# Per-token L2 norms in a delta rule's tables, and a value projection made feature-major

## The reference, cut to what matters

```
q = l2_norm(silu(conv(z_q))) * 128 ** -0.5      # x * rsqrt(sum(x * x) + 1e-6)
k = l2_norm(silu(conv(z_k)))
kk = k @ k.T ;  a_mat = tril(beta * kk * decay, -1) + I
u, w = solve(a_mat, [v * beta, k * beta * exp(gc)])
o = (q * exp(gc)) @ s + (q @ k.T * decay) @ (u - w @ s)
s = s * a_last + (k * exp(gc_last - gc)).T @ (u - w @ s)
y = rms_norm(o_forward + o_backward, g) * silu(gate) @ w_out
```

## Time and profile before

| | us |
|---|---|
| three runs | 3838.85, 3844.15 (median), 3849.88 |
| profiled execution | 3842.82 |
| its span | 3841.0 |

### The profile page before, as it was taken

The page is one execution under the profiler, slowest core; times in us unless marked ns, Lnnn a source line. Parts: engine busy times, 40 slices in busy tenths (PEclk is TensorE's granted clock), DMA queues, the critical chain, the costliest instruction groups (busy, mean ns, idle before and its releaser), DMA issues.

```text
span 3841.0 us, 60563 instructions
## 1 busy us (share of the span) xinstructions
PE 3669.0 (96%) x25450; PEld 2964.8 (77%) x25450; DVE 1940.4 (51%) x3011; ACT 1525.8 (40%) x2592; POOL 841.5 (22%) x829
## 2 busy tenths in 40 slices
PE   7999899999999999999999999999999899999999
PEld 4678787887887667777888788875778688878887
DVE  5656655655444656743344543447565523354343
ACT  5543333433233457634234322235664523343222
POOL 1121232112121225432101121113253211002020
PEclk7999999999999999999999999999999999999999
DMA  6310030032222111111233222220211122322222
GB/s 233 126 51 3 22 69 3 3 121 87 95 99 88 66 39 61 67 45 69 96 108 106 77 99 94 99 72 33 72 61 64 37 99 94 111 87 93 99 99 89
DMA packets 81975, 300.87 MB, mean 78 GB/s; under 512 B 8872, under 2 KB 10024, under 8 KB 81064
## 3 DMA queue, kind: packets, MB, share of 16 engines
q1 hardware_dynamic: 80672, 294.90, 21.8%
q10 hardware_dynamic: 1032, 2.10, 0.5%
HBM read 292.76 MB, written 4.19 MB: 77 GB/s over the span
## 4 chain that ended last, share of the span: by engine, by line
PE 73%; DVE 11%; ACT 6%; issue 5%; POOL 4%; DMA 1%; SPq 0%; DVEq 0%; POOLq 0%; ACTq 0%
PE ps L208 72%; DVE wlo L239 1%; DVE he L247 1%; ACT whi L227 1%; PE ps L213 1%; DVE ac L247 1%; DVE hc L2504 1%; ACT ha L227 1%; POOL p L243 1%; DVE ss L247 1%; ACT wp L228 1%; DVE ha L239 1%; ACT L227 1%; DVE ws L247 1%; DVE sml L1972 1%
## 5 line engine op out<-in xcount | busy, mean ns | idle before, releaser
L239 DVE TENSOR_TENSOR wlo<-wraw,whi 128x1024 fp32r<-128x1024 f32 x537 | 690.5, 1290 | 767.5 <-ACT whi L227 766.9
L208 PE MATMUL ps<-hh,whi 128*128 128x512 f32 x1840 | 729.3, 396 | 7.2 <-ACT hh L227 2.2
L208 PE MATMUL ps<-hh,wlo 128*128 128x512 f32 x1840 | 720.3, 391 | 0.0
L208 PE MATMUL ps<-hl,whi 128*128 128x512 f32 x1840 | 720.3, 391 | 0.0
L227 ACT ACTIVATE whi<-wraw 128x1024 fp32r<-128x1024 f32 x537 | 559.7, 1049 | 214.0 <-PE ps L208 176.9
L208 PEld LDWEIGHTS ps<-hh,whi 128*128 128x128 f32 x1840 | 348.2, 189 | 91.7 <-ACT hh L227 8.7
L208 PEld LDWEIGHTS ps<-hh,wlo 128*128 128x128 f32 x1840 | 347.7, 189 | 73.7
L208 PEld LDWEIGHTS ps<-hl,whi 128*128 128x128 f32 x1840 | 347.9, 189 | 69.8
L208 PE MATMUL ps<-u,u 64*64 64x64 f32 (+1 forms) x6016 | 222.4, 226 | 22.7 <-DVE u L239 16.0
L208 PEld LDWEIGHTS ps<-u,u 64*64 64x64 f32 x6016 | 202.7, 135 | 41.8 <-DVE u L239 18.9
L208 PE MATMUL ps<-gh,wlo 128*128 128x512 f32 x528 | 205.4, 389 | 0.0
(11 more groups left out here) (406 smaller groups left out, 7006.4 us busy)
## 6 DMA issues: line engine op xcount, KB each, us to landing
wraw<-weights SPq DMA_DIRECT2D x537, 512.0 KB, 3.2
x<-xT SPq DMA_DIRECT2D x1, 2048.0 KB, 12.1
bias_lines<-ln ACTq DMA_DIRECT2D x1, 2048.0 KB
x<-xT SPq DMA_DIRECT2D x4, 512.0 KB, 5.3
xmf<-memT SPq DMA_DIRECT2D x2, 1024.0 KB, 4.9
out<-x SPq DMA_DIRECT2D x4, 512.0 KB, 2.6
bias<-bias_lines SPq DMA_DIRECT2D x1, 1536.0 KB, 8.2
con<-consts SPq DMA_DIRECT2D x1, 1379.0 KB, 16.5
```

The costliest lines, as they stand in the source:

```text
L208: self.last, self.open = self.e.matmul(out, lhsT, rhs, start=start, stop=stop, skip_group_check=skip), True
L239: return self.e.tensor_tensor(out, a, b, op)
```

## The change

The norms are no longer applied to queries and keys. `QT`, `KT` and `KM` hold the raw values, and the per-token factors go into tables. With r the reciprocal norm of a key, `beta` (for the values) becomes beta r, `betak` (for the matrix) beta r r, and `nbe` is multiplied by r r. A query's norm is a common factor of its whole output row, and the output is normalized again, so it drops out except beside the epsilon: the sum of squares plus 1e-6, times 128e-6, takes the epsilon's place (`qe`). The sums of the keys' squares are now taken token-major: ScalarE squares the transposed keys out of PSUM, right after it copies them to `KM`, and VectorE reduces them. The powers of a head group's keys are taken together, for 24 columns. The keys' transposes move from step 3 to step 1.

In the window stage the values are projected feature-major, like the keys, copied to `wVT`, and turned by four transposes behind the first scores.

```diff
-    steps = {"q": 3, "k": 4, "v": 2}
+    steps = {"q": 2, "k": 2, "v": 2}
...
@@ pe_chunks
-            elif kind == "v" or step == 3:
+            elif kind != "q":
                 ...
                 K.pe_turn6(z)
-            elif step == 1:
+            else:
                 ... (sums of squares, as before)
-            else:
-                sm = K.sml[("c", *z)]
-                pe.wait_ge(K.pool.at("croot", *z))
-                for m0 in range(0, nt, 4):
-                    b = K.ps.take(pe, "cb", *z, m0)
-                    for m in range(min(4, nt - m0)):
-                        pe.mm(b[:, m * 128:m * 128 + 128], sm[:, m0 + m:m0 + m + 1].broadcast_to([128, 128]), K.con("id"))
-                    pe.mark("cb", *z, m0)
-                pe.also("sml", "c", *z)
@@ pe_turn6
-            pe.wait_ge(K.dve.at("cn", *z, 0), K.dve.at("cn", *z, 4))
+            pe.wait_ge(K.pool.at("cm", *z))
@@ act_chunks
-                if kind != "v":
-                    dst = K.QT[:, i, :] if kind == "q" else K.KT[:, i, :]
+                if kind == "q":
                     act.wait_ge(K.pool.at("cm", *z))
-                    act.a(s[:, 0:nt * 128], dst, ACT.Square).then_inc(act("csq", *z), 1)
+                    act.a(s[:, 0:512], K.QT[:, i, :], ACT.Square).then_inc(act("csq", *z), 1)
...
                     act.cp(dst[:, m0:m0 + mn, i * 128:i * 128 + 128], v).then_inc(act("ct", *z, m0), 1)
+                    if kind == "k":
+                        sq = K.sg[hg][z][:, m0 * 128:(m0 + mn) * 128]
+                        act.a(sq, K.ps[("ct", *z, m0)][:, 0:mn * 128], ACT.Square).then_inc(act("ksq", *z, m0), 1)
@@ dve_chunks (the sums with epsilon and the products "cn" go)
+            elif kind == "q":
+                dve.wait_ge(pe.at("cs", *z), dve.at("qe", 0) if hg else None)
+                dve.ts(K.qsum[:, :, i], K.ps[("cs", *z)][:, 0:4], EPS, ALU.add, 128 * EPS, ALU.mult).then_inc(dve("qsum", hg, i), 1)
+                dve.also("ps", "cs", *z)
+                if i == 3:
+                    K.dve_query_norms(hg)
+            elif kind == "k":
+                dve.wait_ge(K.act.at("ksq", *z, 0), K.act.at("ksq", *z, 4), dve.at("gg"), dve.at("kroot", 0) if hg else None)
+                sq = K.sg[hg][z][:, 0:768].rearrange("p (a b) -> p a b", b=128)
+                dve.e.reduce_sum(K.ksum[:, :, i], sq, AXX).then_inc(dve("ksum", hg, i), 1)
+                dve.also(f"sg{hg}", *z)
+                if i == 3:
+                    dve.wait_ge([dve.at("ksum", hg, j) for j in range(4)])
+                    dve.ts(K.ksum, K.ksum, 1.0, ALU.mult, EPS, ALU.add).then_inc(dve("keps", hg), 1)
+            if (kind, i, step) == ("v", 2, 0):
+                K.dve_key_norms(hg)
@@ pool_chunks (the power and the scaling per item go)
+            elif (kind, i) == ("k", 3):
+                pool.wait_ge(K.dve.at("keps", hg))
+                pool.tt(K.ksum, K.ksum, K.con("mhalf").unsqueeze(2).broadcast_to([128, 6, 4]), ALU.pow).then_inc(pool("kroot", hg), 1)
+    def dve_query_norms(self, hg):      # 4 copies of 64 partitions x 2 x 4 into qe
...
+    def dve_key_norms(self, hg):        # 8 copies of 64 partitions x 2 or 4 x 4 into kroot, then
+        dve.tt(beta, beta, K.kroot, ALU.mult).then_inc(dve("kbeta", hg), 1)
+        dve.tt(nbe, nbe, K.kroot, ALU.mult).then_inc(dve("knbe0", hg), 1)
+        dve.wait_ge(dve.at("knbe0", hg))
+        dve.tt(betak, beta, K.kroot, ALU.mult).then_inc(dve("kbetak", hg), 1)
+        dve.tt(nbe, nbe, K.kroot, ALU.mult).then_inc(dve("knbe", hg), 1)
@@ pool_scan
-                pool.tt(q4(A), q4(E), bcl(K.cols(K.beta, s, hg), 64), ALU.mult).then_inc(pool("eb", *z), 1)
+                pool.tt(q4(A), q4(E), bcl(K.cols(K.betak, s, hg), 64), ALU.mult).then_inc(pool("eb", *z), 1)
@@ dve_osum
-        dve.ts(o[:, 0, hg, j, :], o[:, 0, hg, j, :], 1.0 / 128, ALU.mult, EPS, ALU.add).then_inc(dve("ort", hg, j), 1)
+        dve.stt(o[:, 0, hg, j, :], o[:, 0, hg, j, :], 1.0 / 128, ALU.mult, K.qe[:, hg, j, :], ALU.add).then_inc(dve("ort", hg, j), 1)
@@ pe_window
-        K.projT(("wv", l), [("w_in_2", l, k * 128, slice(o, o + 128)) for k in ks8], 128,
-                [(b[:, c * 128:c * 128 + 128], c == 0) for c in range(4)], h)
+        K.proj(("wv", l), K.win(l, "v", 0), [(ps.take(pe, "wv", l), h)])
...
+            if c == 0:                  # behind the first eight score products' banks
+                b = ps.take(pe, "wvt", l)
+                pe.wait_ge(act.at("wvT", l))
+                for n in range(4):
+                    pe.tr(b[:, n * 128:n * 128 + 128], L.wVT[:, n * 128:n * 128 + 128], K.con("id"))
+                pe.mark("wvt", l)
@@ act_window
-        act.wait_ge(pe.at("wv", l))
-        act.cp(L.wV.rearrange("p a b -> p (a b)"), ps["wv", l]).then_inc(act("wv", l), 1)
+        act.wait_ge(pe.at("wv", l), K.ended("units", l))
+        act.cp(L.wVT, ps["wv", l]).then_inc(act("wvT", l), 1)
         act.also("ps", "wv", l)
+        act.wait_ge(pe.at("wvt", l))
+        act.cp(L.wV.rearrange("p a b -> p (a b)"), ps["wvt", l]).then_inc(act("wv", l), 1)
+        act.also("ps", "wvt", l)
```

More of the change, by code:

```diff
@@ L492, in layout @@
         self.nbe = self.sb("nbe", G, [128, 2, 6, 8])
+        self.qe = self.sb("qe", G + 160, [128, 2, 4, 4])
+        self.ksum = self.sb("ksum", G + 384, [128, 6, 4])
+        self.kroot = self.sb("kroot", G + 408, [128, 2, 6, 4])
+        self.betak = self.sb("betak", G + 480, [128, 2, 6, 8])
+        self.qsum = self.sb("qsum", G + 976, [128, 4, 4])
         self.ea = self.sb("ea", G + 960, [128, 2, 8])
@@ L600, in layout @@
             L.wV = self.sb("wv", M + 2560, [128, 4, 128])
+            L.wVT = self.sb("wvt", M + 9216, [128, 512])
             L.wS = self.ring(f"ws{l}", [self.sb("ws", M + o, [128, 4, 384]) for o in (3072, 4608, 12288)], after_b)
@@ L1264, in dve_chunks @@
                     K.dve_osum(0, i, K.OT[:, i, 1, :])
[L1265 to L1270, removed]
-                dve.also("ps", "cs", *z)
[L1272 to L1279, removed]
+            elif kind == "q":
+                dve.wait_ge(pe.at("cs", *z), dve.at("qe", 0) if hg else None)
+                dve.ts(K.qsum[:, :, i], K.ps[("cs", *z)][:, 0:4], EPS, ALU.add, 128 * EPS, ALU.mult).then_inc(dve("qsum", hg, i), 1)
+                dve.also("ps", "cs", *z)
+                if i == 3:
[10 more added lines that the diff above has]
+                K.dve_key_norms(hg)
             if (hg, kind, i, step) == (0, "q", 2, 1):
@@ L1317, in pool_chunks @@
                     pool.also(f"ac{hg}", *z)
[L1318 to L1325, removed]
-        pool.mark("end", "chunks", hg)
+            elif (kind, i) == ("k", 3):
+                pool.wait_ge(K.dve.at("keps", hg))
+                pool.tt(K.ksum, K.ksum, K.con("mhalf").unsqueeze(2).broadcast_to([128, 6, 4]), ALU.pow).then_inc(pool("kroot", hg), 1)
+        pool.mark("end", "chunks", hg)
+    def dve_query_norms(self, hg):
+        K, dve = self, self.dve
+        dve.wait_ge([dve.at("qsum", hg, i) for i in range(4)], K.act.at("beta"), dve.at("da"))
+        for half in range(2):
+            r = slice(64 * half, 64 * half + 64)
+            for first in range(2):
+                tiles = K.qsum[r, 0:2, :] if first == half else K.qsum[r, 2:4, :][:, ::-1, :]
+                dve.cp(K.qe[r, hg, first::2, :], tiles).then_inc(dve("qe", hg), 1)
+    def dve_key_norms(self, hg):
+        K, dve = self, self.dve
+        heads = slice(hg * 4, hg * 4 + 4)
+        dve.wait_ge(K.pool.at("kroot", hg), dve.at("nbe"), K.act.at("beta"))
+        for half in range(2):
+            r = slice(64 * half, 64 * half + 64)
+            for par in range(2):
+                for lo, hi in ((0, 2), (2, 6)):
+                    tiles = K.ksum[r, lo:hi, :] if par == half else K.ksum[r, lo:hi, :][:, ::-1, :]
+                    dve.cp(K.kroot[r, par, lo:hi, :], tiles).then_inc(dve("kroot", hg), 1)
+        beta, nbe, betak = (x[:, :, :, heads] for x in (K.beta, K.nbe, K.betak))
+        dve.wait_ge(dve.at("kroot", hg))
+        dve.tt(beta, beta, K.kroot, ALU.mult).then_inc(dve("kbeta", hg), 1)
[3 more added lines that the diff above has]
+        dve.tt(nbe, nbe, K.kroot, ALU.mult).then_inc(dve("knbe", hg), 1)
     def pair(self, s):
@@ L2696, in pe_window @@
         K.proj(("wk", l), K.win(l, "k", 0), [(ps.take(pe, "wk", l), h)])
-        b = ps.take(pe, "wv", l)
-        o = WIN_COLS["v"]
-        K.projT(("wv", l), [("w_in_2", l, k * 128, slice(o, o + 128)) for k in ks8], 128,
-                [(b[:, c * 128:c * 128 + 128], c == 0) for c in range(4)], h)
+        K.proj(("wv", l), K.win(l, "v", 0), [(ps.take(pe, "wv", l), h)])
         rows = [slice(64 * e, 64 * e + 64) for e in range(2)]
```

## The result

The changed kernel takes 3812.6 us (median of 4 runs, 3808.7 to 3814.0) against 3847.0 for the kernel before (4 runs): a ratio of 0.991, interval 0.9897 to 0.9923, 34 us less. The forecast was 3811. The profiled execution's span fell from 3841.0 to 3808.7 us, by 32.3; the forecast sum was 32.4.

What follows compares the result with a forecast made beforehand. TensorE, busy 96% of the span, was taken as the bound. Head group 1 (13.2), head group 0 (14) and the windows (5.2) sum to 32.4 us off 3842.8, so 3810.4, predicted as 3811; range 3800 to 3826.

Steps and rivals of the forecast that it cites:

- TensorE's issue time: Chunk stages: removed spreads and sums of keys (20.8 us) and spreads of queries (7.1 us) free 27.9 us of TensorE's queue.
- the loop beside TensorE: Key chunks of head group 1: the loop bound by ScalarE falls from about 10.9 to 9.8 us, against TensorE's 9.2.
- Head group 1: Chunk stage at 455 to 585 us, without modulation weights: last value's copy of z at 561.8 instead of 575.01, gain 13.2 us.
- Head group 0: Chunk stage at 60 to 262 us, with modulation weights: 14 us off, between 3.9 and 18, depending on waits for `wlo`.
- The added wait: Key chunks: VectorE's reduction waits for ScalarE's squares ahead of the next `wlo`, which TensorE needs; hidden with 2.4 us slack.
- Small operations and the power: Chunk stages: twelve small VectorE operations and GpSimd's 24-column power (about 5 us) cost 0, at worst 0.8 us per head group.
- The windows: Start of window attention, two layers: feature-major value projection takes 2.6 us off each, 5.2 us; bounds 0 and 2 x 4.7.
- The key products on GpSimd: Key chunks: the new order avoids the port lock with VectorE's `wlo`, some 0.6 us per such chunk; left out of the sum.
- A: Rival, chunk stages and windows: the waits go as well, 43 us off, 3800 us; chance 0.16.
- B: Rival: feeders bind, saving ahead of modulation waits is refilled (4 us left), 17 us off in all, 3826 us; chance 0.18.
- C: Rival, slower: VectorE's reduction holds `wlo` back beyond the slack in all 8 key chunks, 3855 us; chance 0.03.

Runs made afterwards that it cites:

- the repeated squares: Changed kernel with every square of a transposed key done twice or four times on ScalarE: 3816.7 us (ratio 0.9929) and 3835.2 us (0.9976).
- win_only: The kernel before with only the window's value projection changed to feature-major with four transposes: 3839.0 us, ratio 0.9986 to the kernel before, 4.4 us less.
- filling products: Changed kernel with transposes behind the gate projection, plus constant products in five kinds of TensorE's idle places: 3808.2 us, ratio 0.9908 to the kernel before.

## Why the prediction was right

Point by point, by its own steps.

- **TensorE's issue time is worth its full length.** Shown for the keys: putting their 20.8 us back cost 20. For the whole, 27.9 us were counted and the norm part gave 29. It holds only because the loop beside TensorE got shorter too, from about 10.9 to 9.5 us per key chunk, as the prediction had it.
- **Head group 1, 13.2 us forecast, 15.2 measured (16.7 in the second profile).** The steps written down in the prediction end at 561.5, not 561.8, so its own walk gives 13.5. Of the other 1.7 us, 1.1 lie behind the first key and 0.6 ahead of it. The loop was right in kind (shown by the repeated squares) and 0.3 us too long, 9.8 for 9.5 per key chunk: the copies and squares overlap more, 508.09 to 509.57 = 1.48 us where 1.8 was taken. The prediction ran the loop over the copy of z, though; it goes over the low part on VectorE. Ahead of the first key, TensorE's idle before the third query's sums was 2.13 us instead of about 3. (In the sum for the loop of before, 0.76 for the sigmoid is a slip for 0.86; with it the sum is the stated 10.9, and the convolutions there start 10.87 us apart, 520.91 and 531.78.)
- **Head group 0, 14 forecast, 13.7 measured from first to last copy of z.** The waits for `wlo` were not refilled: 11.3 us before and after, 9.7 in the second profile, whose stage is 11.7 us shorter. The absolute end of the last value's copy moved less, from 250.88 to 239.71, since this profile entered the stage 2.6 us later.
- **The added wait is hidden.** Right that TensorE doesn't wait for `wlo` in the key chunks of group 1: the block is ready at 502.5 and wanted at mid-projection, near 505.7 (the next block's DMA is issued at 505.90, when TensorE has let one go), 3.2 us of slack instead of 2.4. But the wait was not the added risk that it was taken for. VectorE waited there for ScalarE's high part already, and the reduction ends 0.1 us after that part. The sum in the prediction, by way of ScalarE, was right; its words, that the low part hangs on the reduction, were not.
- **Small operations and the power at no cost.** Right, but narrowly: the 24-column power took 5.06 us (5 forecast). The twelve small operations took 3.1 us of VectorE (544.54 to 547.64), where 3 us of room were forecast; behind them and a weight split VectorE still waited 0.30 us for the last copy of z.
- **The windows, 5.2 forecast, 3.8 in `win_only`, 2.3 and 3.6 in the changed kernel's two profiles.** The mis-sized term. The first score operation moved by 2.7 us as forecast, but nothing was counted behind it. The transposes' and the next bank's waits (1.3 to 1.7 + 0.9 us) stand in front of the gate projection, and the gate ran at the slow clock for part of its length (7.2 to 7.3 us; 8.6 in layer 1 of the first profile), 5.7 at full clock. With the transposes moved it is 5.0 us in all.
- **The key products on GpSimd.** The prediction's remark, left out of its sum, came true in group 0: the pairs of products took 1.98, 2.67, 1.99 and 3.02 us before and 1.96 to 2.00 after. ScalarE no longer waits for them, and no run shows what it is worth.
- **Rivals.** A (all waits go as well, 43 us) failed in group 0, where the waits for `wlo` stayed, and in the windows; in group 1 it was near, with 16 us against 15.2 and 16.7 measured. B (feeders refill) failed in group 0. C (slower) wanted the squares 6.5 us later. With the squares 3 us longer 25 of the 34 us are gone, but mostly through the loop: TensorE's waits for `wlo` grew from 4.5 to 7.6 us in group 0 (130 to 250 us) and stayed away in group 1. So the loop's price comes first.
- **The total: partly luck.** Group 0 was 0.3 us too high, group 1 2.0 too low, the windows 2.9 too high, which leaves 13.7 + 15.2 + 2.3 = 31.2. The remaining 1.1 of the 32.3 us is what is left of -2.6 (start), +0.5, -2.9, +4.1 and +2.0 us, in stretches in which the kernels are alike. Such stretches differ by microseconds between profiles (from the last copy of z to the first window 1109.1 us before, up to 1113.3 in the others). What is shown is the size of the gain in the chunk stages, not a forecast good to 1 us.

## What to carry to other kernels

Where TensorE is the bound, count the distance between starts of the small products that only carry scalars around, and look whether the scalar can go into a table that is read anyway. Then write down the loop of the engines beside it, operation by operation: it is what the next microsecond taken from TensorE runs into. Follow it by what each operation really waited for; here the weight split on VectorE was in it and the copy of z was not, and no run has tried to take the split out. A short product that needs a bank still held by a slower engine made a window 0.3 to 2.3 us longer when it stood ahead of the next long projection instead of behind it (traces without filling products; the times alone don't settle it).

## What the hardware showed that I had not expected

In the changed kernel one of the four small table products on VectorE took nine times as long as its neighbours, while GpSimd's product ran (VectorE, then GpSimd). It is no accident of one profile: in both head groups of all ten profiles with the changed keys it took 1.81 to 1.85 us.

```profile
545.52 0.20 DVE L239 TENSOR_TENSOR nbe<-nbe,kroot 128x48 f32<-128x48 f32 x1
545.76 1.84 DVE L239 TENSOR_TENSOR betak<-beta,kroot 128x48 f32<-128x48 f32 x1
547.52 0.20 DVE L239 TENSOR_TENSOR nbe<-nbe,kroot 128x48 f32<-128x48 f32 x1
```

```profile
545.65 1.88 POOL L239 TENSOR_TENSOR ac<-ac,sg 128x772 f32<-128x772 f32 x1 [6.87 <-ACT sg L227]
```

GpSimd's starts first, at 545.65, and ends at 547.53; VectorE's ends at 547.60. The Trainium skill, SBUF — State Buffer, section "SBUF: two separate sides", says that the ports which both engines share are an exclusive lock between a VectorE operation with two SBUF inputs and a GpSimd operation that reads SBUF, held by whoever starts first for its whole instruction. The trace agrees: the tiny operation, whose neighbours of the same size take 0.20 us, ends with the other one. Here it was hidden, with 0.30 us to spare.

The start of the kernel differs by 8.7 us between profiles with identical instructions there: the first copy of z stands at 68.1 to 76.8 us. It doesn't wholly go through: the changed kernel's second profile starts 8.4 us earlier than its first, but group 0 takes 165.0 us instead of 162.9 (0.5 us more in the queries, 1.9 between the fourth key and the second value). What sets the start no run shows.
